# Attention: the low half of an output block subtracted one step later on VectorE

## What is computed

```python
def causal_block_attention(q, k, v, scale):
    S = q.shape[1]
    outs = []
    for blk in range(S // Q_BLOCK):
        q0 = blk * Q_BLOCK
        kend = q0 + Q_BLOCK
        qb = q[:, q0:kend]
        s = jnp.einsum('bqhd,bkhd->bhqk', qb, k[:, :kend]).astype(jnp.float32) * scale
        mask = jnp.arange(kend)[None, :] <= (q0 + jnp.arange(Q_BLOCK))[:, None]
        s = jnp.where(mask, s, jnp.float32(-1e30))
        prob = jax.nn.softmax(s, axis=-1).astype(v.dtype)
        outs.append(jnp.einsum('bhqk,bkhd->bqhd', prob, v[:, :kend]))
    return jnp.concatenate(outs, axis=1)
```

## Time and profile before

| | |
|---|---|
| median of 3 runs | 3448.19 us (3447.79 to 3449.36) |
| time of the profiled execution | 3451.54 us |
| its span in the profile | 3450.2 us |
| TensorE busy (matmul) | 3348.3 us, 97% |
| VectorE busy | 2058.9 us, 60% |
| ScalarE busy | 1384.1 us, 40% |
| GpSimd busy | 1318.0 us, 38% |

### The profile page before, as it was taken

The page is one execution under the profiler, slowest core; times in us unless marked ns, Lnnn a source line. Parts: engine busy times, 40 slices in busy tenths (PEclk is TensorE's granted clock), DMA queues, the critical chain, the costliest instruction groups (busy, mean ns, idle before and its releaser), DMA issues.

```text
span 3450.2 us, 48917 instructions
## 1 busy us (share of the span) xinstructions
PE 3348.3 (97%) x19926; PEld 2727.8 (79%) x19926; DVE 2058.9 (60%) x2697; ACT 1384.1 (40%) x2360; POOL 1318.0 (38%) x698
## 2 busy tenths in 40 slices
PE   7999999999989999999999999999999999999999
PEld 6788888897668778878887777777788878888887
DVE  4656737427764743335556548986545578888554
ACT  4443434344543544431114447772223344444212
POOL 3212222110024444454442126663344356666542
PEclk9999999999999999999999999999999999999999
DMA  5101111010036344452222232223456433333422
GB/s 156 41 19 47 43 33 48 26 56 14 1 98 208 128 129 137 133 183 98 98 98 98 99 103 67 84 83 109 153 186 191 124 98 104 116 111 122 176 97 81
DMA packets 343791, 344.40 MB, mean 100 GB/s; under 512 B 14661, under 2 KB 263937, under 8 KB 343568
## 3 DMA queue, kind: packets, MB, share of 16 engines
q1 hardware_dynamic: 328960, 307.00, 28.1%
q10 hardware_dynamic: 11520, 25.17, 1.9%
q0 software_dynamic: 3088, 9.10, 0.7%
HBM read 268.86 MB, written 72.35 MB: 99 GB/s over the span
## 4 chain that ended last, share of the span: by engine, by line


## 5 line engine op out<-in xcount | busy, mean ns | idle before, releaser
L462 POOL TENSOR_TENSOR weight_lo<-stage,weight_hi 128x1024 fp32r<-128x1024 f32 (+4 forms) x269 | 625.0, 2331 | 970.8 <-ACT weight_hi L439 942.0
L2478 DVE TENSOR_TENSOR x<-x,psum 128x512 f32<-128x512 f32 x416 | 284.3, 687 | 280.6 <-PE psum L403 269.7
L439 ACT ACTIVATE weight_hi<-stage 128x1024 fp32r<-128x1024 f32 (+4 forms) x329 | 299.4, 924 | 315.2 <-PE psum L403 274.5
L401 PE MATMUL psum<-hT_hi,weight_hi 128*128 128x512 f32 x1024 | 412.4, 403 | 1.5 <-DVE hT_lo L658 1.5
L402 PE MATMUL psum<-hT_lo,weight_hi 128*128 128x512 f32 x1024 | 401.6, 392 | 0.0
L403 PE MATMUL psum<-hT_hi,weight_lo 128*128 128x512 f32 x1024 | 401.3, 392 | 0.0
L401 PE MATMUL psum<-weight_hi,act_hi 128*128 128x512 f32 x864 | 338.4, 392 | 3.9 <-POOL act_lo L2426 2.1
L402 PE MATMUL psum<-weight_lo,act_hi 128*128 128x512 f32 x864 | 337.9, 391 | 0.0
L403 PE MATMUL psum<-weight_hi,act_lo 128*128 128x512 f32 x864 | 337.6, 391 | 0.0
L462 POOL TENSOR_TENSOR weight_lo<-sum,weight_hi 128x512 fp32r<-128x512 f32 (+1 forms) x114 | 240.2, 2117 | 232.9 <-ACT weight_hi L439 232.9
L401 PE MATMUL psum<-T_hi,weight_hi 128*128 128x512 f32 x608 | 238.3, 392 | 6.2 <-DVE U L2336 5.1
(11 more groups left out here) (423 smaller groups left out, 7112.6 us busy)
## 6 DMA issues: line engine op xcount, KB each, us to landing
stage<-in_w_up SPq DMA_DIRECT2D x66, 512.0 KB, 4.4
stage<-in_w_in SPq DMA_DIRECT2D x64, 512.0 KB, 4.0
act_raw<-scratch_act SPq DMA_DIRECT2D x54, 512.0 KB, 5.4
stage<-in_w_ffn_up SPq DMA_DIRECT2D x48, 512.0 KB, 4.6
scratch_gates<-gate ACTq DMA_DIRECT2D x64, 256.0 KB, 2.0
gs<-scratch_gates SPq DMA_DIRECT2D x64, 256.0 KB, 3.0
stage<-in_w_out SPq DMA_DIRECT2D x32, 512.0 KB, 4.6
scratch_act<-out SPq DMA_DIRECT2D x64, 256.0 KB, 4.5
```

The costliest lines, as they stand in the source:

```text
L401: q.matmul(out, stat[0], mov[0], start=first, stop=False, skip_group_check=onto)
L439: a.q.activation(hi[:, part], src, ACT.Copy).then_inc(*S.w_hi.up(w))
L462: g.q.tensor_tensor(lo[:, part], src, hi[:, part].bitcast(F32), ALU.subtract).then_inc(*S.w_lo_pool.up(w))
L2478: v.q.tensor_tensor(dst, dst, K.bank(key), ALU.add).then_inc(*S.x.up(("f", f, g, t, n)))
```

## The change

VectorE's part of the step `output` becomes a step of its own, `output_low`, with the same function. It is issued for unit u in loop step u+4 instead of u+3, right behind `scale_p`, so ahead of the transposes' copy of that step. TensorE and ScalarE keep their parts of `output` where they were. The loop gets one more step so that the last unit's low half is still issued.

```diff
--- before.py
+++ after.py
@@ -3594,7 +3594,7 @@
     o.do("kpe_rope")
     advance(first, NT + 6)
     feed, fed = iter(()), 0
-    for i in range(len(UNITS) + TURN_LAG + OUT_LAG):
+    for i in range(len(UNITS) + TURN_LAG + OUT_LAG + 1):
         if i < len(UNITS):
             pair = UNITS[i][0]
             if i % (2 * NT) == 0:
@@ -3609,11 +3609,14 @@
         advance(feed, more)
         if 0 <= i - 1 < len(UNITS):
             o.do("scale_p", i - 1)
+        u = i - 1 - TURN_LAG - OUT_LAG
+        if u >= 0 and UNITS[u][1]:
+            o.do("output_low", u)
         if 0 <= i - TURN_LAG < len(UNITS):
             o.do("turn_p", i - TURN_LAG)
         advance(feed, more)
         u = i - TURN_LAG - OUT_LAG
-        if u >= 0 and UNITS[u][1]:
+        if 0 <= u < len(UNITS) and UNITS[u][1]:
             o.do("output", u)
         advance(feed, more)
         if i < len(UNITS):
@@ -4162,7 +4165,7 @@
-            "head_turn": dve_head_turn, "score": dve_score, "scale_p": dve_scale_p, "turn_p": dve_turn_p, "output": dve_output,
+            "head_turn": dve_head_turn, "score": dve_score, "scale_p": dve_scale_p, "turn_p": dve_turn_p, "output_low": dve_output,
```

## The result

The changed kernel takes 3472.66 us (median of 4 runs, 3468.37 to 3480.53), the kernel before 3448.16: a ratio of 1.0066, 95% interval 1.0054 to 1.0077. It is slower, by 24.5 us where 17.3 were forecast, and it lies above the range. Three more series gave 1.0060 (1.0047 to 1.0073), 1.0068 (1.0056 to 1.0081) and 1.0058 (1.0045 to 1.0072) against the kernel before on the same chip, that is 20.9, 23.0 and 21.1 us. The range reached to 21.3 us over the kernel before, so two of these three would have lain just inside it: a part of the miss is the scatter of the first series.

A forecast was written before the change was run, and what follows sets the result against it. The prediction took the attention stage to be bound by a ring of three in-order engines. Delays of 7.0, 4.9, 2.85 and 2.55 us summed to 17.3, added to the median for 3465.5 us; range 3458.5 to 3469.5.

The forecast's parts named there:

- The bound and the mechanism: Attention stage: three in-order engines in a ring; TensorE's second block waits in bank 7 for the first's moved low half.
- What is removed is worth nothing: VectorE's 18.9 us wait for ScalarE's high half goes, but waiting for scores takes it back: gain 0, at most 0.2 elsewhere.
- The terms of the sum: Delays of TensorE's second block by groups of attention steps: 7.0, 4.9, 2.85 and 2.55 us, together 17.3.
- The slack of steps 6, 22 and 38: VectorE reaches step 6 earlier by more than the block's 0.48 us delay; taken as 0, bounds 0 and 0.48 each.
- The sum is the whole change of the time: The attention stage's 17.3 us added to the median gives the new time, 3465.5 us; what follows keeps its length.
- rival C: TensorE's new idle stretches halve its clock in attention: about 1.8 us each, 16 us more at nine steps, 3482; chance 5%.
- The argument against C: TensorE's new attention stretches, 1.6 to 1.75 us, are no longer than old ones (up to 2.0) and lie between full bursts.
- D: Time doesn't change: TensorE's wait is for something earlier than the low half, or VectorE's queue isn't moved; chance 4%.
- A: The attention ring has unseen slack that mostly absorbs the delay: half the sum, 8.6 us, time 3456.8; chance 12%.
- B: Faster: removing VectorE's wait brings rotations and additions in attention forward, 9 us less, 3439; chance 4%.
- steps 10, 26 and 42: Steps with the next pair's projections: block 1.43 us late, 0.82 of it slack, about 0.85 left each, 2.55 together.
- step 54: Attention step whose block comes 1.67 us late; at most 1.44 arrives, since the exponential had stood 0.23; taken as 1.35.

The follow-up runs named there:

- two_banks_after: The changed kernel with output blocks alternating between PSUM banks 6 and 7, and transposes and projections on three banks instead of four: 3451.62 us, ratio 1.0006.
- large_only: Against the kernel before, only the low half of the large block of each pair is moved: 3468.82 us, ratio 1.0054.
- small_only: Against the kernel before, only the low half of the small block of each pair is moved: 3450.39 us, ratio 1.0002.
- after: The changed kernel in its first series, with its first profile: 3472.66 us, ratio 1.0066.
- again: The changed kernel repeated unchanged, on a chip where the kernel before took 3450.63 us: 3471.57 us.
- again_2: The changed kernel repeated unchanged, beside the kernel before on the same chip: 3472.62 us, ratio 1.0068.
- again_3: The changed kernel repeated unchanged, beside two kernels with added matmuls and the kernel before at 3449.68 us: 3470.79 us.
- three filled kernels: The changed kernel plus unread matmuls in nine new TensorE waits (3466.40 us), also in steps 10, 26, 42 (3467.68), or also in steps 17, 33, 49 (3461.77).
- both filler kernels: The changed kernel plus unread matmuls ahead of the second output block in nine steps (3466.40 us), or also in steps 10, 26, 42 (3467.68 us).

## Why the forecast was missed

By its own steps:

- *The bound and the mechanism*: right. Bank 7 ties TensorE's second block to the first one's low half; two_banks_after removes all but 0.9 us of the 17.0 with the order kept, and large_only has 16.3 of them.
- *What is removed is worth nothing*: right. VectorE's wait for the high half fell from 18.9 to 2.1 us, the tail's, and its wait for scores rose from 29.9 to 60.8 us. small_only gains nothing.
- *The terms of the sum*: right, 17.0 us against 17.3, each group within 0.11 us. The slack of steps 6, 22 and 38 was there: VectorE comes to the mask of unit 6 earlier by 0.56 us, and TensorE goes on unchanged. The earlier trace rows gave both terms.
- *The sum is the whole change of the time*: wrong, and here is the failing step: rival C, the clock. It was given 5% and a price of all nine steps at once (16 us), and what it would do in part was left out of the range. In the four profiles of the changed kernel it came in two or three places of the stage, 4.6 to 6.2 us in all. The price of one fall, 1.8 us, was about right: 1.6 to 1.7 was measured for most. That it would come in a few steps and not in all or none was what the prediction lacked.
- *The argument against C*: "the new stretches are no longer than the old ones". True, and no argument: the old ones lose the clock as well, only not in the one execution that was profiled. The second profile of the same kernel has two such places. A profile without a fall behind a 1.7 us wait shows that the fall need not come, not that it can't.
- *D, A and B* did not occur. A's slack was found only where the sum had it: 0.90 us in steps 10, 26 and 42 (0.82 forecast) and some 0.3 in step 54.

How the excess divides is shown only in part. In four profiles the changed kernel has 6.1, 4.6, 6.2 and 6.2 us at half clock in the stage (after, again, again_2, again_3), the kernel before 0 and 3.3 in two. By place, in the same order:

| us at half clock in the stage | after | again | again_2 | again_3 |
|---|---|---|---|---|
| behind new waits (steps 14, 30, 54, 58) | 2.9 | 0 | 4.6 | 4.5 |
| behind the old waits of steps 17, 33, 49 | 3.2 | 1.6 | 1.6 | 1.6 |
| at units 2 to 4, ahead of the first moved low half | 0 | 3.0 | 0 | 0 |

The nine new waits of 1.55 us and more in each profile make 36; behind 8 of them the clock fell. In the three filled kernels it fell behind none of 27. So the first row is the change's, 3.0 us on average. The second has its like in the kernel before. The third stands ahead of everything that the change moves, and small_only and both filler kernels have it too.

By the profiles the stage grew by 22.8 us on average against the first profile of before, and by some 21 against the mean of its two. The medians of the later three series say 20.9 to 23.0, so little is left to explain there. The 24.5 of the first series is higher, with four executions of the changed kernel from 3468.4 to 3480.5 us and of the kernel before all within 1.6 us; single executions of the latter took 3442.7 to 3457.4 us over the later series. What the first series has above that, no profile places.

## To carry to other kernels

Before moving an evacuation back in a queue, look for who reuses its buffer next and when. A wait that can be seen to end on the engine itself (VectorE's 18.9 us) may be covered by what comes after it, while the bank's next user has no cover at all. The price is then read from two rows, the start of the next user and the new end of the evacuation, less the slack of whoever stands behind.

Where a change puts new idle stretches like these into TensorE's stream, count their half clock as a likely extra with its own part of the range, at the price of one or a few falls, and take a second profile of the kernel before you call its clock steady.

## What the hardware showed

- The granted clock fell to a half (1.2 GHz) behind single waits of 1.60 to 1.73 us in an otherwise full stream (891.29, 981.19 and 830.47 above), in some executions and not in others, at the same instruction. Why it falls in one execution and not in the next is not shown.
- A fall cost 1.6 to 1.7 us where scores of a large unit stood behind it, and 2.9 us for the two of steps 54 and 58 together. Large scores that take 1.98 us at full clock took 2.22 to 3.13 behind the old waits, the output block of 20 records 1.81 to 2.40 instead of 1.31.
- Doing more can be faster: matmuls that nobody reads, in twelve waits of 1.55 to 1.73 us, took 9.0 us off the changed kernel by the medians (3470.79 to 3461.77). Of these, 6.4 us are seen in the profiles of the stage, where the granted clock stayed at 1.00; where the other 2.6 lie is not shown.
